# First norm of a two-layer diffusion trunk: whose engine makes the low parts of the first weight chunks, and in which order VectorE and TensorE take the tiles

## The chip, the cores and the metric

One core of one Trainium2 chip runs the whole program. The metric is the device time of one execution in microseconds (us). Names used here: TensorE (PE in the profile, PEld its weight loads), VectorE (DVE), ScalarE (ACT), GpSimd (POOL), and SyncE (SP), which issues most of the DMAs.

## The reference, cut to what matters

Two trunk layers on 256 latent and 256 context tokens of width 1024. Each layer is a half-step SwiGLU, a token mixer and a second half-step SwiGLU. Ahead of each stands an RMS norm with an adaptive shift and scale, which are themselves products of a conditioning vector with a weight matrix:

```python
ml = _split_mod(cond_lat @ mod_w[i] + mod_b[i])
mc = _split_mod(cond_ctx @ mod_w[i] + mod_b[i])
h = h + 0.5 * ml[2] * _swiglu(_modulate(h, ml[0], ml[1]), ffn1_w13[i], ffn1_w2[i])

def _modulate(h, shift, scale):
    return _rms(h) * (1.0 + scale) + shift
def _swiglu(h, w13, w2):
    a, b = jnp.split(h @ w13, 2, axis=-1)
    return (jax.nn.silu(a) * b) @ w2
```

The place of the change is the very first `_modulate` and the first columns of `h @ w13` behind it.

## The kernel before, in words

Activations lie transposed: eight tiles (k = 0 to 7) of 128 partitions (features) by 512 columns (256 latent, 256 context tokens). Every operand of a large product is split in two fp32r parts, a high part (a rounded copy) and a low part ("rest", the value less the high part), and each product is made of three: high weight by high x (`wh`, `xh`), low weight by high x (`wl`, `xh`), high weight by low x (`wh`, `xl`). ScalarE makes the high parts (casts), VectorE the rests (subtractions). Weights come in chunks of 1024 rows by 256 columns, each in two pieces of 128 x 1024 elements. Chunks 0 and 1 (the first pair) and chunk 2 are loaded before the steady loop begins. Chunks 0 and 1 are cut by halves of the rows: pieces 0 and 1 (rows 0 to 511, first gate and first value columns) lie in `raw`, pieces 2 and 3 (rows 512 to 1023) in `modw`; chunk 2 goes to `extra_hi` and `extra_lo` (inside `uh`).

The first norm runs tile by tile, and four engines take part in each tile k:

- `start_products(k)` on VectorE: two column sums (L872, two inputs of 128 x 1024 from SBUF) that make the scale of tile k, and a small operation (L1004) that finishes it.
- `start_tile(("shift", k))` on TensorE: eight fp32 products of two columns each (L1473, 16 instructions in the trace) that make the shift of tile k. `start_shift(k)` on VectorE (L1013) takes it out of PSUM.
- `start_tile(k)` on VectorE (L1037): x tile times the spread norm factors. It reads one operand in SBUF and one in PSUM.
- ScalarE: `xh` of tile k (L653, two halves), then the same in full precision in `tmp` (L659, two halves).
- `start_lo(k)` on VectorE (L1045): `xl` = `tmp` less `xh`, two inputs in SBUF.
- `start_products(k)` on TensorE: 12 products of 512 columns (L1486 and L1487 in turn, then four of L1492, which need `xl`).

TensorE's own order is: spread of the factors (L1676), shift sum of tile 1, then for each k: shift sum of tile k + 1, the 12 products of tile k. The order on every engine is the order of the code; engines meet at counting semaphores. `hi_ready` counts casts of weight pieces, `lo_ready` rests. GpSimd has only one thing to do in this stage, the root of the norm factors (L498), and behind it the fetches of the next modulation weights into `modw` (L522), which wait for `lo_ready` of 4 because pieces 2 and 3 lie in the same memory.

Behind the norm comes the "up" stage: chunk 2 (`extra_hi`, `extra_lo`), chunk 3, and then a loop over pairs of chunks, about 22 us each. In its first pair VectorE makes four column sums on the fetched modulation weights (`late_unit`), then the products of the two branches (L1164), their rests (L1169) and the rests of chunk 3 (L860).

Of the kernel before, what the change touches and what calls it, by code (L numbers as in the profile page):

```python
# [6 lines left out]
ALU = mybir.AluOpType  # L7
ACT = mybir.ActivationFunctionType
AX = mybir.AxisListType
F32 = mybir.dt.float32  # L10
# [156 lines left out]
def trunk(nc, tokens, columns, cond_rows, row_params, mod_start, mod_rows, f1_w13, f1_w2, f2_w13, f2_w2,  # L167
# [8 lines left out]
    with ExitStack() as stack:  # L176
# [313 lines left out]
        def _(pool):  # L490
# [14 lines left out]
            for ph in phases:  # L505
# [3 lines left out]
                elif kind == "norm" and ph["n"] == 0:  # L509
                    pool.wait_ge(ones_ready, 2)  # L510
                    root(0, slice(0, TT))
                elif kind == "norm":
                    for half in range(ph["T"] // LAT):
                        root(ph["st"] + half, slice(half * LAT // P, (half + 1) * LAT // P))
# [45 lines left out]
        def _(act):  # L560
# [78 lines left out]
            for n_ph, ph in enumerate(phases):  # L639
# [3 lines left out]
                if kind == "norm":  # L643
                    n, m0 = ph["n"], ph["L"] * MODT + 3 * ph["sub"] * DT
                    if n == 0:
                        for k in range(DT):
# [16 lines left out]
                            if k >= DT - 2:  # L663

                                p = k - (DT - 2)
# [185 lines left out]
        def _(dve):  # L851
# [11 lines left out]
            def start_pieces(p):  # L863
                for s in range(2):
                    cut = slice(p * DT // 2, (p + 1) * DT // 2)
                    dve.wait_ge(hi_ready, 2 * p + s + 1)
                    nc.vector.tensor_tensor(flat(wl[:, s, cut]), modw_slot[:, s] if p else raw[:, s, :],
                                            flat(wh[:, s, cut].bitcast(F32)), ALU.subtract).then_inc(lo_ready, 1)

# [154 lines left out]
            for n_ph, ph in enumerate(phases):  # L1024
# [9 lines left out]
                elif kind == "norm" and ph["n"] == 0:  # L1034
# [3 lines left out]
                    def extra_rest(p):  # L1038
                        half = slice(p * DT // 2, (p + 1) * DT // 2)
                        dve.wait_ge(hi_ready, 5 + p)  # L1040
                        nc.vector.tensor_tensor(flat(extra_lo[:, half]), raw[:, p, :], flat(extra_hi[:, half].bitcast(F32)),
                                                ALU.subtract).then_inc(lo_ready, 1)
# [4 lines left out]
                    start_pieces(0)  # L1047
                    start_products(1)
# [3 lines left out]
                    for k in range(1, 3):  # L1052
                        start_tile(k)
                    for k in range(1, DT):
                        start_shift(k)
                        start_lo(k - 1)
                        if k == 3:
                            start_pieces(1)
                        if k + 1 < DT:
                            start_products(k + 1)  # L1060
                        if k + 2 < DT:
                            start_tile(k + 2)
                        if k == DT - 1:
                            extra_rest(0)
                    start_lo(DT - 1)
                    extra_rest(1)
# [66 lines left out]
                elif kind == "up":  # L1133
# [6 lines left out]
                    def pair(i, units, unit_first=False):  # L1140
# [30 lines left out]
                        rest(2 * (q0 + i + 1) + 1, 1, late=late)  # L1171
                    pair(0, False, unit_first=ph["units"] > 0)
# [726 lines left out]
```

## Time and profile before

| | us |
|---|---|
| median of 3 runs | 1901.37 (1899.33 to 1901.51) |
| the profiled execution | 1904.52 |
| its span, first to last instruction | 1902.6 |
| TensorE busy | 1850.8 (97% of the span) |
| VectorE busy | 1185.4 (62%) |
| ScalarE busy | 687.8 (36%) |
| GpSimd busy | 149.6 (8%) |

The span is divided by stage in the trace; the stage of the change is its first 63 us. The granted clock of TensorE has two levels, 2.4 GHz (shown as 1.00) and 1.2 GHz. A matmul of 512 columns starts every 0.23 us at the high level and every 0.43 us at the low one. Over the span the mean is 0.987.

### The profile page before, as it was taken

How to read it: one execution, taken by the hardware profiler on the slowest of the kernel's cores; microseconds unless marked ns; L12 is line 12 of the kernel's file. 1: busy time of each engine (PE TensorE's matmuls, PEld its weight loads, DVE VectorE, ACT ScalarE, POOL GpSimd, SP SyncE). 2: the span in 40 equal slices, each digit the busy share in tenths (PEclk: the TensorE clock that was granted, in tenths of full speed). 3: DMA queues.
4: the chain of work that ended last, by engine and by line, in shares of the span. 5: the costliest groups of instructions: out<-in, count | busy, mean ns of one | idle time of the engine just before them, and what ended most of it. 6: DMA issues, size and time to landing. Idle time of an engine off the chain costs nothing.

```text
span 1902.6 us, 27442 instructions
## 1 busy us (share of the span) xinstructions
PE 1850.8 (97%) x9984; PEld 1587.8 (83%) x9984; DVE 1185.4 (62%) x1898; ACT 687.8 (36%) x1152; POOL 149.6 (8%) x228
## 2 busy tenths in 40 slices
PE   8999999999989999999999999999999989989997
PEld 6888888898966888888889888888898879978886
DVE  7877772355478478777424887752377445667764
ACT  5332232233258243223223322322254323545552
POOL 0010000100301200011001001000100000010000
PEclk9999999999999999999999999999999989999999
DMA  8466643334510246565233566533343213545554
GB/s 320 148 206 196 194 150 107 92 106 158 145 55 1 67 155 199 189 196 184 91 104 98 178 213 195 187 113 92 99 151 108 69 46 111 177 155 177 193 167 127
DMA packets 81886, 271.85 MB, mean 143 GB/s; under 512 B 9489, under 2 KB 14865, under 8 KB 81809
## 3 DMA queue, kind: packets, MB, share of 16 engines
q1 hardware_dynamic: 62354, 201.58, 32.4%
q0 software_dynamic: 19456, 69.22, 12.1%
q8 instruction: 52, 0.85, 0.2%
q14 instruction: 24, 0.20, 0.0%
HBM read 267.62 MB, written 1.05 MB: 141 GB/s over the span
## 4 chain that ended last, share of the span: by engine, by line
PE 90%; DVE 5%; issue 2%; ACT 2%; DMA 1%; SPq 0%; POOL 0%; POOLq 0%; DVEq 0%; ACTq 0%
PE pt L1429 19%; PE pt L1430 19%; PE pt L1432 19%; PE pt L1404 9%; PE pt L1403 4%; PE pt L1622 2%; PE pt L1839 2%; PE pt L1841 2%; PE pt L1840 2%; DVE wl L860 1%; PE pt L1502 1%; PE pt L1626 1%; PE pt L1566 1%; PE pt L1721 1%; PE pt L1568 1%
## 5 line engine op out<-in xcount | busy, mean ns | idle before, releaser
L860 DVE TENSOR_TENSOR wl<-raw,wh 128x1024 fp32r<-128x1024 f32 (+2 forms) x394 | 432.0, 1135 | 411.6 <-ACT wh L571 407.3
L1429 PE MATMUL pt<-xh,wh 128*128 128x512 f32 (+1 forms) x1312 | 496.5, 378 | 3.3 <-DVE wl L860 3.1
L1430 PE MATMUL pt<-xh,wl 128*128 128x512 f32 (+1 forms) x1312 | 495.2, 377 | 0.0
L1432 PE MATMUL pt<-xl,wh 128*128 128x512 f32 (+1 forms) x1312 | 493.8, 377 | 0.0
L571 ACT CAST wh<-raw 128x1024 fp32r<-128x1024 f32 (+2 forms) x394 | 364.2, 970 | 281.5 <-PE pt L1432 148.5
L872 DVE CUSTOM_DVE_ANT_0 pt<-modw,raw 128x1024 f32<-128x1024 f32 x256 | 305.7, 1253 | 17.4 <-DMA modw<-in_mod_rows 17.3
L1429 PEld LDWEIGHTS pt<-xh,wh 128*128 128x128 f32 x1312 | 248.4, 189 | 48.5 <-issue 3.7
L1432 PEld LDWEIGHTS pt<-xl,wh 128*128 128x128 f32 x1312 | 248.3, 189 | 45.5
L1430 PEld LDWEIGHTS pt<-xh,wl 128*128 128x128 f32 x1312 | 248.5, 189 | 44.6
L720 ACT CAST uh<-tmp 128x512 f32 (+3 forms) x88 | 49.7, 567 | 293.3 <-DVE tmp L1164 284.8
L1430 PE MATMUL pt<-uh,wl 128*128 128x512 f32 x396 | 154.1, 389 | 0.0
L1429 PE MATMUL pt<-uh,wh 128*128 128x512 f32 x396 | 154.1, 389 | 0.0
L1432 PE MATMUL pt<-ul,wh 128*128 128x512 f32 x396 | 154.1, 389 | 0.0
L1404 PE MATMUL pt<-xh,wh 128*128 128x512 f32 x352 | 121.7, 399 | 2.2 <-issue 2.2
L522 POOL DMA_DIRECT2D modw<-in_mod_rows x128 | 68.0, 531 | 642.4 <-DVE small L872 617.5
L710 ACT ACTIVATE tmp<-pt 128x512 f32<-128x512 f32 x66 | 39.1, 597 | 184.9 <-PE pt L1432 181.9
L1430 PEld LDWEIGHTS pt<-uh,wl 128*128 128x128 f32 x396 | 74.4, 188 | 15.5
L1432 PEld LDWEIGHTS pt<-ul,wh 128*128 128x128 f32 x396 | 74.3, 188 | 15.4
L1429 PEld LDWEIGHTS pt<-uh,wh 128*128 128x128 f32 x396 | 74.3, 188 | 15.3
L1403 PE MATMUL pt<-xh,wl 128*128 128x256 f32 x308 | 86.3, 280 | 0.0
L504 POOL TENSOR_TENSOR tmp<-tmp 128x512 f32<-128x512 f32 (+1 forms) x36 | 39.8, 1106 | 582.7 <-ACT tmp L578 582.5
L1404 PEld LDWEIGHTS pt<-xh,wh 128*128 128x128 f32 x352 | 63.7, 190 | 14.7 <-issue 2.5
(222 smaller groups left out, 2782.5 us busy)
## 6 DMA issues: line engine op xcount, KB each, us to landing
raw<-in_ffn_w SPq DMA_DIRECT2D x238, 512.0 KB, 4.0
modw<-in_mod_rows POOLq DMA_DIRECT2D x128, 512.0 KB, 4.6
raw<-in_ret_w_in SPq DMA_DIRECT2D x48, 512.0 KB, 4.5
raw<-in_diff_w_in SPq DMA_DIRECT2D x24, 512.0 KB, 4.4
raw<-in_ffn_w SPq DMA_DIRECT2D x32, 256.0 KB, 3.9
raw<-in_ret_w_out SPq DMA_DIRECT2D x16, 512.0 KB, 4.4
region<-in_mod_rows SPq DMA_DIRECT2D x8, 512.0 KB, 14.6
region<-in_mod_start SPq DMA_DIRECT2D x8, 512.0 KB, 15.0
```

The lines of the kernel that those rows point to most:

```text
L504: nc.gpsimd.tensor_tensor(ssq[:, 0:T], ssq[:, 0:T], tmp[:, e % 2, 0:T], ALU.add).then_inc(sq_added, 1)
L522: pool.dma_start(modw_slot[:, e], src).then_inc(mod_landed[e], 16)
L571: nc.scalar.copy(flat(wh[:, s, k0:k0 + part_rows]), raw[:, slot, 0:part_rows * CW]).then_inc(hi_ready, 1)
L710: nc.scalar.activation(tmp[:, t, 0:T], pt[:, t, 0:T], ACT.Silu).then_inc(evac[0], 1)
L720: nc.scalar.copy(row(uh, 2 * i + t)[:, 0:T], tmp[:, 2 + t, 0:T]).then_inc(u_hi_done, 1)
L860: nc.vector.tensor_tensor(flat(wl[:, s, cut]), raw[:, raw_slot(late, s, p), 0:part_rows * CW], flat(wh[:, s, cut].bitcast(F32)), ALU.subtr ...
L872: return nc.vector.tensor_tensor_reduce(products[j], weights, cond_row[:, j, :], 1.0, 0.0, ALU.mult, ALU.add, dst)
L1403: nc.tensor.matmul(bank[:, 0:LAT], w_lo, both[:, 0:LAT], start=False, stop=False)
L1404: ins = nc.tensor.matmul(bank, w_hi, both, start=a, stop=b)
L1429: nc.tensor.matmul(bank, w_hi[:, k, cut], hi(k), start=a, stop=False)
L1430: nc.tensor.matmul(bank, w_lo[:, k, cut], hi(k), start=False, stop=False)
L1432: return nc.tensor.matmul(bank, w_hi[:, k, cut], lo(k), start=False, stop=b)
```

## The change

The six rests of the pieces of chunks 0, 1 and 2 move from VectorE to GpSimd, as 128 x 1024 subtractions behind its root. VectorE normalises tile 0 as soon as the factors are spread, ahead of the column sums for tile 1, and then each tile k + 1 ahead of the column sums for tile k + 1. TensorE makes the four `wh` by `xh` products of a tile first, then the four `wl` by `xh`. ScalarE casts the two pieces of chunk 2 one tile earlier. VectorE waits for all six rests before its first own one.

```diff
                     pool.wait_ge(ones_ready, 2)
                     root(0, slice(0, TT))
+                    for p in range(2):
+                        for s in range(2):
+                            cut = slice(p * DT // 2, (p + 1) * DT // 2)
+                            pool.wait_ge(hi_ready, 2 * p + s + 1)
+                            nc.gpsimd.tensor_tensor(flat(wl[:, s, cut]), modw_slot[:, s] if p else raw[:, s, :],
+                                                    flat(wh[:, s, cut].bitcast(F32)), ALU.subtract).then_inc(lo_ready, 1)
+                    for p in range(2):
+                        half = slice(p * DT // 2, (p + 1) * DT // 2)
+                        pool.wait_ge(hi_ready, 5 + p)
+                        nc.gpsimd.tensor_tensor(flat(extra_lo[:, half]), raw[:, p, :], flat(extra_hi[:, half].bitcast(F32)),
+                                                ALU.subtract).then_inc(lo_ready, 1)
...
-                            if k >= DT - 2:
+                            if k in (DT - 3, DT - 2):
 
-                                p = k - (DT - 2)
+                                p = k - (DT - 3)
                                 act.wait_ge(raw_landed[p], 16 * raw_count(False, 1, 0))
...
-                    start_pieces(0)
-                    start_products(1)
                     dve.wait_ge(bcast_ready, 1)
                     start_tile(0)
                     start_shift(0)
-                    for k in range(1, 3):
-                        start_tile(k)
+                    start_tile(1)
+                    start_products(1)
                     for k in range(1, DT):
                         start_shift(k)
                         start_lo(k - 1)
-                        if k == 3:
-                            start_pieces(1)
                         if k + 1 < DT:
+                            start_tile(k + 1)
                             start_products(k + 1)
-                        if k + 2 < DT:
-                            start_tile(k + 2)
-                        if k == DT - 1:
-                            extra_rest(0)
                     start_lo(DT - 1)
-                    extra_rest(1)
...
+                    if q0 == 0:
+                        dve.wait_ge(lo_ready, 6)
                     pair(0, False, unit_first=ph["units"] > 0)
...
             def start_products(d):
 
                 halves = TOK // LAT
+                p = d // (DT // 2)
+                pe.wait_ge(hi_ready, 2 * p + 2)
+                pe.wait_ge(x_hi_done, halves * (d + 1))
                 for s in range(2):
-                    pe.wait_ge(lo_ready, 2 * (d // (DT // 2)) + s + 1)
-                    if s == 0:
-                        pe.wait_ge(x_hi_done, halves * (d + 1))
                     for t in range(2):
                         cut, bank = slice(t * P, (t + 1) * P), pt[:, 2 * s + t, :]
                         nc.tensor.matmul(bank, wh[:, s, d, cut], xh[:, d, :], start=(d == 0), stop=False)
+                for s in range(2):
+                    pe.wait_ge(lo_ready, 2 * p + s + 1)
+                    for t in range(2):
+                        cut, bank = slice(t * P, (t + 1) * P), pt[:, 2 * s + t, :]
                         nc.tensor.matmul(bank, wl[:, s, d, cut], xh[:, d, :], start=False, stop=False)
```

On GpSimd's queue, behind the root, the fetches of modulation weights stood next before:

```order
L498 TENSOR_TENSOR small<-small 128x4
L522 DMA modw<-in_mod_rows 128x1024
L522 DMA modw<-in_mod_rows 128x1024
L534 UNCONDITIONAL_BRANCH
L534 ISA
```

and stand behind the six rests now:

```order
L498 TENSOR_TENSOR small<-small 128x4 [waits var_ready,ones_ready]
L516 TENSOR_TENSOR wl<-raw,wh 128x1024 [waits hi_ready] x2
L516 TENSOR_TENSOR wl<-modw,wh 128x1024 [waits hi_ready] x2
L521 TENSOR_TENSOR uh<-raw,uh 128x1024 [waits hi_ready] x2
L533 DMA modw<-in_mod_rows 128x1024 [waits lo_ready]
L533 DMA modw<-in_mod_rows 128x1024
```

So both fetches are issued only after the last rest of chunk 2.

On VectorE's queue, from the scale of tile 0 to the low part of tile 0, this stood before (`region<-region,raw` is a column sum, `wl<-raw,wh` a rest, `region<-hT,pt` a normalised tile, `modT<-pt,cols_in` a shift):

```order
L1004 TENSOR_SCALAR sc<-small,cols_in 128x2
L867 TENSOR_TENSOR wl<-raw,wh 128x1024 x2
L872 ISA region,small<-region,raw 128x1024
L872 ISA small 128x1
L872 ISA region,small<-region,raw 128x1024
L872 ISA small 128x1
L1004 TENSOR_SCALAR sc<-small,cols_in 128x2
L1037 TENSOR_TENSOR region<-hT,pt 128x512
L1013 TENSOR_SCALAR modT<-pt,cols_in 128x2
L1037 TENSOR_TENSOR region<-hT,pt 128x512 x2
L1013 TENSOR_SCALAR modT<-pt,cols_in 128x2
L1045 TENSOR_TENSOR xl<-tmp,xh 128x512
```

and this stands there now:

```order
L1008 TENSOR_SCALAR sc<-small,cols_in 128x2
L1041 TENSOR_TENSOR region<-hT,pt 128x512
L1017 TENSOR_SCALAR modT<-pt,cols_in 128x2
L1041 TENSOR_TENSOR region<-hT,pt 128x512
L876 ISA region,small<-region,raw 128x1024
L876 ISA small 128x1
L876 ISA region,small<-region,raw 128x1024
L876 ISA small 128x1
L1008 TENSOR_SCALAR sc<-small,cols_in 128x2
L1017 TENSOR_SCALAR modT<-pt,cols_in 128x2
L1044 TENSOR_TENSOR xl<-tmp,xh 128x512
```

The two rests are gone, the first tile and its shift stand ahead of the column sums of tile 1, and the low part still stands behind the shift of the next tile.

## Rows read from the trace of the kernel before

**Rows 1.** Granted clock and busy time by stretch (engines' us, PEclk, DMA share, GB/s).

```profile
40.00:50.00 10.00, 9.41 (x38) 7.64 (x37) 8.76 (x20) 4.15 (x8) 0.00 (x0) 0.71 0.26 101
```

**Rows 2.** Timeline of TensorE, tiles 0 and 1: start us, us, line, operation.

```profile
19.59 3.54 PE L1473 MATMUL pt<-cond,region 128*128 128x2 f32 x16
24.17 0.77 PE L1486 MATMUL pt<-xh,wh 128*128 128x512 f32 x1 [1.03 <-ACT xh L653]
...
28.37 1.84 PE L1473 MATMUL pt<-cond,region 128*128 128x2 f32 x16
30.07 0.47 PE L1486 MATMUL pt<-xh,wh 128*128 128x512 f32 x1
...
32.00 1.09 PE L1492 MATMUL pt<-xl,wh 128*128 128x512 f32 x4
32.92 1.84 PE L1473 MATMUL pt<-cond,region 128*128 128x2 f32 x16
```

**Rows 3.** Timeline of TensorE, end of tile 3 to chunk 2.

```profile
40.85 0.39 PE L1487 MATMUL pt<-xh,wl 128*128 128x512 f32 x1
41.82 1.19 PE L1492 MATMUL pt<-xl,wh 128*128 128x512 f32 x4 [0.58 <-DVE xl L1045]
42.85 2.20 PE L1473 MATMUL pt<-cond,region 128*128 128x2 f32 x16
44.91 0.77 PE L1486 MATMUL pt<-xh,wh 128*128 128x512 f32 x1
...
50.18 2.24 PE L1473 MATMUL pt<-cond,region 128*128 128x2 f32 x16
...
62.64 0.47 PE L1429 MATMUL pt<-xh,uh 128*128 128x512 f32 x1
```

**Rows 4.** Timeline of VectorE: column sums, tile, rests.

```profile
14.47 1.23 DVE L872 CUSTOM_DVE_ANT_0 region<-region,raw 128x1024 f32<-128x1024 f32 x1
...
25.65 1.22 DVE L872 CUSTOM_DVE_ANT_0 region<-region,raw 128x1024 f32<-128x1024 f32 x1
...
28.19 0.68 DVE L1037 TENSOR_TENSOR region<-hT,pt 128x512 f32<-128x512 f32 x1
...
35.54 2.36 DVE L867 TENSOR_TENSOR wl<-modw,wh 128x1024 fp32r<-128x1024 f32 x2
```

**Rows 5.** Timeline of ScalarE: high part of tile 0, casts of pieces 2 and 3.

```profile
22.93 1.09 ACT L653 ACTIVATE xh<-region,modT,sc 128x256 fp32r<-128x256 f32 x2 [5.14 <-DVE modT L1013]
...
32.54 1.97 ACT L629 CAST wh<-modw 128x1024 fp32r<-128x1024 f32 x2
```

**Rows 6.** GpSimd's groups by shape: busy us, mean ns, idle before.

```profile
L504 POOL TENSOR_TENSOR tmp<-tmp 128x512 f32<-128x512 f32 x24 | 31.0, 1291 | 333.6 <-ACT tmp L578 333.4
L504 POOL TENSOR_TENSOR tmp<-tmp 128x256 f32<-128x256 f32 x12 | 8.8, 736 | 249.1 <-ACT tmp L578 249.1
```

**Rows 7.** Timeline of GpSimd at 632 us, and VectorE's L860 there.

```profile
632.86 2.73 POOL L504 TENSOR_TENSOR tmp<-tmp 128x512 f32<-128x512 f32 x2 [10.45 <-ACT tmp L578]
...
L860 DVE TENSOR_TENSOR wl<-raw,wh x1: 2144/2144/2144, 634.5 to 634.5; 128x1024 fp32r<-128x1024 f32 x1
```

**Rows 8.** VectorE's L860 over the whole span: ns min/median/max, first and last start.

```profile
L860 DVE TENSOR_TENSOR wl<-raw,wh x394: 410/1219/2144, 69.7 to 1884.8; 128x1024 fp32r<-128x1024 f32 x197
```

**Rows 9.** GpSimd's root of 128x4 elements, and the eight others of its shape.

```profile
14.65 1.91 POOL L498 TENSOR_TENSOR small<-small 128x4 f32<-128x4 f32 x1 [13.54 <-DVE small L892]
...
L554 POOL TENSOR_TENSOR small<-small x8: 1006/1008/1030, 566.9 to 620.9; 128x4 f32<-128x4 f32 x8
```

**Rows 10.** One of those eight, and VectorE beside it.

```profile
576.00 1.01 POOL L554 TENSOR_TENSOR small<-small 128x4 f32<-128x4 f32 x1 [8.09 <-DVE small L1302]
...
575.84 0.74 DVE L1315 SCALAR_TENSOR_TENSOR xl<-pt,small,xh 128x512 fp32r<-128x512 f32 x1
```

**Rows 11.** Fetches of modulation weights: GpSimd's timeline, and their landing.

```profile
38.21 1.27 POOL L522 DMA_DIRECT2D modw<-in_mod_rows  x2 [21.64 <-DVE wl L867]
...
modw<-in_mod_rows POOLq DMA_DIRECT2D x2, 512.0 KB, 4.4
```

More of the change, by code:

```diff
@@ L861, in rest @@
                                             flat(wh[:, s, cut].bitcast(F32)), ALU.subtract).then_inc(lo_ready, 1)
[L863 to L868, printed above, removed]
             def column_sum(dst, weights, j, products):
@@ L1037, in start_tile @@
                         nc.vector.tensor_tensor(start_sq[k], hT[:, k, :], pt[:, BC, :], ALU.mult).then_inc(normed, 1)
[L1038 to L1042, printed above, removed]
                     def start_lo(k):
```

## The prediction

> **What bounds the kernel now.** I read the chain of waits first: 90% of it is TensorE, so what TensorE gains by 62.64 us, where chunk 2 begins, it keeps to the end, as long as nothing behind is late. Then the stretches: the stage of the change holds one with a low clock, 0.71 on average from 40 to 50 us [rows 1]. Then TensorE's timeline. A full tile has a pitch of 4.55 us (28.37 to 32.92): 1.70 for the shift sum of the next tile and 2.85 for the 12 products, of which the last four, which need `xl`, begin 1.93 after the first [rows 2]. Against that pitch three things are lost. (a) TensorE is free at 23.13 (19.59 + 3.54) and waits 1.03 for `xh` of tile 0 [rows 2]. (b) At tile 3 the last `wl` product starts at 40.85, so `xl` is due at 41.08; it comes at 41.82: 0.74 [rows 3]. (c) Behind this stall and the nearly empty shift sum TensorE runs at 1.2 GHz: the 12 products of tile 4 take 5.27 (44.91 to 50.18) instead of 2.85, the two shift sums around them 2.20 and 2.24 instead of 1.84 [rows 2, 3], together 3.2.
>
> Why is VectorE late at tile 3? Its work per tile is 2.54 for the column sums (25.65 to 28.19 [rows 4]), about 0.60 each for tile and low part (half of a 1024 rest) and 0.13 for the shift: 3.9 of the 4.55. That leaves it 0.7 in hand, and the two rests at 35.54 take 2.3 [rows 4]. Other rests stand where VectorE waits anyway.
>
> **The change part by part.** *Start.* VectorE no longer makes two rests and the sums of tile 1 before tile 0. The factors are spread when TensorE turns to the shift sum at 19.59, so `xh` is ready at about 21.7 (0.7 for tile and shift, 1.1 on ScalarE [rows 2, 5]), before 23.13. TensorE starts 1.03 earlier; part of that is spent in products at the low clock, which I expect to rise at the same moment as before. I take -0.6; the bound is -1.03.
>
> *Rests off VectorE.* Without them VectorE keeps the pace, and (b) and (c) go: -0.74 and -3.2. With the start -4.5, the most this change can bring (-5.0 with the bound above).
>
> *Rests on GpSimd.* 128x256 takes it 736 ns, 128x512 1291 [rows 6], 555 for each 256 elements, so 128x1024 should take 2.40, six of them 14.4. GpSimd has nothing else to do here. By its own clock the rests are in time: pieces 2 and 3 are cast by about 33.9 and would be ready at 38.7, and the `wl` products of tile 4 need them at about 44.
>
> But the two engines do not work side by side. At 634.53 VectorE's L860 starts while GpSimd is in the second of two additions of 128x512, which end at 635.59 (632.86 + 2.73). It takes 2144 ns [rows 7] where the median is 1219 [rows 8]: 0.93 more for 1.06 of overlap. The other way round, GpSimd's root, started 0.18 after a column sum, takes 1.91, and operations of its shape take 1.01 [rows 4, 9]; 0.9 is what was left of the column sum. Beside a VectorE operation with one input in PSUM GpSimd isn't delayed (1.01 [rows 10]). So I read: GpSimd's two-input operations and VectorE's operations on two SBUF inputs exclude each other, each waits for the end of the other's instruction, and normalised tiles and shifts run on. Column sums and low parts, 3.1 of VectorE's 3.9 per tile, are of the kind that waits. The Trainium skill says the same in its GPSIMD Engine Reference, section Specifications: the SBUF interfaces are shared with VectorE, with contention when that has two SBUF inputs. By its figure of 4497 ns for 2048 elements (section Performance versus the Vector engine) a rest would be an estimated 2.25; the sum uses 2.40.
>
> I follow the timetable with this rule; t(k) is the time at which TensorE turns to the products of tile k - 1. Tile 0 ends at about 27.8 (28.37 - 0.6), so t(2) = 27.8 + 1.7 = 29.5 and t(3) = 29.5 + 4.55 = 34.05. The first two rests fall where VectorE waits for the spread and cost it 0.5 with room to spare. The third starts at 33.2, behind a column sum, and ends at 35.65. VectorE wants the low part of tile 2 at 34.3 and gets it at 36.2; it is due at 34.05 + 1.93 = 35.98: stall 0.2. The fourth rest follows to 38.5 and holds the column sums of tile 4, which end at 41.0; the low part of tile 3 stands behind them and is there at 41.85, due at t(4) + 1.93 = 38.8 + 1.93 = 40.7: stall 1.15. VectorE catches up at tile 4. The fifth rest (cast at 48.3, run 48.85 to 51.25) puts the low part of tile 5 at 51.75 against 51.0: stall 0.8. The sixth (cast 52.3) falls among the column sums of tile 7, and the low part of tile 6 comes at 58.0 against 56.3: stall 1.75. Sum of the stalls +3.9; tile 7 ends at about 61.8. Bounds: 0 if the engines run side by side, and 6.5 if VectorE must let two rests in a row pass (2.4 more at tile 2, with a little recovered at tile 3).
>
> *Clock.* In the trace a stall of 0.74 beside a shift sum was followed by one low stretch worth 3.2. The new timetable has three stalls of that size or larger beside a shift sum, so I expect one low stretch again. But while TensorE is slow VectorE catches up, and one or two of the later stalls shrink by about 2.0 together. Net +1.2; bounds 0 (none) and 6.4 (two stretches, nothing recovered).
>
> *Order on TensorE, casts.* The `wh` products in front make `wl` due 0.9 later; it isn't what is late in the walk. The casts of chunk 2 fill ScalarE's idle time and end before the fifth and sixth rests need them. Both cost nothing; if `wl` of tile 4 were late after all, the four `wh` products cover 0.9.
>
> *Fetches.* They stand behind six rests now and are issued at 56 instead of 38.21 (1.27 for both), and land 4.4 later [rows 11], at about 61.5. The four column sums of the first up pair then end near 66.5, chunk 3's first rest near 70.5, due at 61.8 + 0.24 + 48 x 0.2275 = 73.0. The cover is about 2.5; the price nothing now, one for one beyond it. VectorE's new wait for six rests ends earlier than the landing. SyncE's loads of chunk 3 wait for rests 5 and 6, which come at 51 and 56 and so no later than before.
>
> Sum against the profiled execution (1904.52, span 1902.6): -4.5 + 3.9 + 1.2 = +0.6. The profile is 3.15 above the median of the timed runs, which is close to what its low stretch cost. If timed runs mostly lack that stretch, their start is only 1.3 better than now at best, and the same new stalls and one stretch make +3.8 (-1.3 + 3.9 + 1.2). I take a value nearer to the profile than to this end: +1.0, so 1902.4.
>
> **The rivals.** 0.2 per cent (3.8 us) is about what a measurement of this kernel tells from no change.
>
> Likeliest (0.60): exclusion as above, the stall on `xl` moved from one place to three or four. 1902.4, its own range 1899.5 to 1905.5.
>
> Side by side (0.20): GpSimd's long subtractions pass between VectorE's operations, TensorE has no stall, no low stretch: 1901.4 - 4.5 = 1896.9, or 1900.1 against runs that had no low stretch. For it: GpSimd is idle here. Against it: 2144 against 1219.
>
> Clock falls twice (0.15), the one on the slower side: the stalls of 1.15 and 1.75 are each followed by a low stretch, whose 3.2 is not recovered because the second comes last. 1901.4 - 4.5 + 3.9 + 6.4 = 1907.2. It decides from a second stretch on; for it speaks that the new stalls are longer than the 0.74 that was followed by one, against it that stretches overlap stalls.
>
> Late fetches (0.05): exclusion delays the rests and so the fetches by 5 more, over the cover of 2.5: TensorE waits 2.5 at chunk 3, 1904.9.
>
> **How the numbers follow.** Faster by over 0.2% is the better half of side by side plus an edge of the likeliest: 0.15. Slower is the two falls and an edge of the likeliest and of late fetches: 0.18. The rest, 0.67, is within 0.2%. The range leaves out half of side by side and half of the two falls: 1898.0 to 1905.8.
>
> **What would show it.** In the profile after: the six rests at 2.4 each or longer; column sums or low parts on VectorE with 2 to 3 us instead of 1.22 and 0.68 where a rest overlaps; TensorE waiting for `xl` at tiles 2, 3, 5 and 6; `xh` of tile 0 no longer waited for; chunk 2 begun at 61 to 63. The prediction is wrong if VectorE's maxima stay at 1.2 and chunk 2 begins near 58, or if GpSimd's rests stretch over 5 us and TensorE waits for `wl`.

## The result, and the profile after

| | before | after |
|---|---|---|
| median, us (20 runs each) | 1901.26 (1898.72 to 1904.71) | 1906.34 (1902.05 to 1910.43) |
| ratio of after to before | | 1.0022, 95% interval 1.0015 to 1.003 |
| profiled execution, us | 1904.52 | 1907.78 |
| its span, us | 1902.6 | 1905.8 |
| chunk 2 begins at, us | 62.64 | 65.77 |
| GpSimd busy, us | 149.6 | 164.5 |
| VectorE busy, us | 1185.4 | 1189.4 |

The changed kernel is slower, by 0.22 per cent by the ratio, which is just over what this measurement can tell from no change; the medians lie 5.1 apart (0.27 per cent). Its runs fall in two groups, 9 from 1902.05 to 1903.75 and 11 from 1906.24 to 1910.43, and the profile is from the second. Two of the rows need a word. GpSimd's 14.9 more are the six subtractions. VectorE's busy time has grown although its work shrank: time in which an instruction of VectorE is held by GpSimd counts as its busy time.

In the two profiles the whole loss lies ahead of chunk 2: it begins 3.13 later and the span is 3.2 longer. TensorE's timeline of the changed kernel, stage of the change:

```profile
19.83 3.54 PE L1466 MATMUL pt<-cond,region 128*128 128x2 f32 x16 [0.17 <-DMA region<-in_mod_start]
23.24 2.05 PE L1479 MATMUL pt<-xh,wh 128*128 128x512 f32 x4
...
27.78 1.84 PE L1466 MATMUL pt<-cond,region 128*128 128x2 f32 x16
...
35.05 1.07 PE L1484 MATMUL pt<-xh,wl 128*128 128x512 f32 x4
38.51 1.20 PE L1489 MATMUL pt<-xl,wh 128*128 128x512 f32 x4 [2.39 <-DVE xl L1044]
39.54 2.48 PE L1466 MATMUL pt<-cond,region 128*128 128x2 f32 x16
41.88 2.05 PE L1479 MATMUL pt<-xh,wh 128*128 128x512 f32 x4
...
47.14 1.96 PE L1466 MATMUL pt<-cond,region 128*128 128x2 f32 x16
...
55.87 1.20 PE L1489 MATMUL pt<-xl,wh 128*128 128x512 f32 x4 [0.27 <-DVE xl L1044]
...
61.74 1.19 PE L1489 MATMUL pt<-xl,wh 128*128 128x512 f32 x4 [1.04 <-DVE xl L1044]
...
65.77 0.47 PE L1422 MATMUL pt<-xh,uh 128*128 128x512 f32 x1
```

It answers to [rows 2, 3]. `xh` of tile 0 is no longer waited for: the second shift sum starts at 27.78 instead of 28.37. Tile 2 waits for `xl` until 38.51, where it was due at 34.04 + 1.93 = 35.97: 2.5 lost. Tiles 5 and 6 lose 0.4 and 1.2 more by the same count. Behind the longest stall TensorE falls to its lower clock, and the 12 products of tile 3 take 5.26 (41.88 to 47.14) instead of 2.85. By stretch, the granted clock stands in the column behind the five engines, and answers to [rows 1]:

```profile
30.00:40.00 10.00, 7.61 (x44) 6.30 (x43) 9.96 (x11) 6.01 (x10) 4.84 (x2) 1.00 0.91 361
40.00:50.00 10.00, 10.00 (x46) 8.66 (x46) 6.36 (x16) 2.63 (x6) 0.00 (x0) 0.66 0.00 2
```

In the first stretch TensorE is busy for 7.61 of 10 and VectorE for 9.96 with 11 instructions; in the second it is the other way round, VectorE has 3.6 to spare. GpSimd's timeline says what ran beside it:

```profile
16.56 4.83 POOL L516 TENSOR_TENSOR wl<-raw,wh 128x1024 fp32r<-128x1024 f32 x2
33.06 4.84 POOL L516 TENSOR_TENSOR wl<-modw,wh 128x1024 fp32r<-128x1024 f32 x2 [11.67 <-ACT wh L640]
52.54 2.54 POOL L521 TENSOR_TENSOR uh<-raw,uh 128x1024 fp32r<-128x1024 f32 x1 [14.63 <-ACT uh L678]
58.40 2.55 POOL L521 TENSOR_TENSOR uh<-raw,uh 128x1024 fp32r<-128x1024 f32 x1 [3.32 <-ACT uh L678]
60.89 1.27 POOL L533 DMA_DIRECT2D modw<-in_mod_rows  x2
```

And VectorE's timeline, at the third and fourth rest and at the first fetched weights:

```profile
33.40 2.21 DVE L1008 TENSOR_SCALAR sc<-small,cols_in 128x2 f32<-128x2 f32 x1
35.53 0.21 DVE L1017 TENSOR_SCALAR modT<-pt,cols_in 128x2 f32<-128x2 f32 x1
35.66 2.79 DVE L1044 TENSOR_TENSOR xl<-tmp,xh 128x512 fp32r<-128x512 f32 x1
...
66.92 1.23 DVE L876 CUSTOM_DVE_ANT_0 pt<-modw,raw 128x1024 f32<-128x1024 f32 x1 [2.34 <-DMA modw<-in_mod_rows]
```

The third rest starts at 33.06 beside a column sum that ends at 33.36. The next instruction on VectorE is the small one that finishes a scale (L1008, 128 x 2 elements, one tensor input): it starts at 33.40 and is held until the third rest ends at 35.5. The shift (L1017, input in PSUM) takes its usual 0.21. Then the fourth rest has begun, and the low part, which TensorE waits for, is held for its whole length: 2.79 instead of 0.68. The three other rests that meet a scale (the first, the fifth and the sixth) hold it the same way. The group view of L1008 and L1044 (ns minimum/median/maximum):

```profile
L1008 DVE TENSOR_SCALAR sc<-small,cols_in x8: 228/1208/2229, 16.9 to 58.7; 128x2 f32<-128x2 f32 x8
...
L1044 DVE TENSOR_TENSOR xl<-tmp,xh x8: 674/682/2795, 23.9 to 63.3; 128x512 fp32r<-128x512 f32 x8
```

The fetches leave at 60.89, VectorE waits 2.34 for what they bring, and chunk 3 begins without a wait all the same. At no place of this stage does TensorE wait for `wl`, so GpSimd is not simply too slow.

### The profile page after: what moved, and what is told of

Its sections match the earlier page's. It is cut to its first block, busy times and chain, and to the rows that moved or that the text cites. A ratio compares the mean times of both kernels' runs of the same rounds, so it can differ in the third digit from the quotient of the medians.

```text
span 1905.8 us, 27443 instructions
## 1 busy us (share of the span) xinstructions
PE 1851.5 (97%) x9984; PEld 1587.6 (83%) x9984; DVE 1189.4 (62%) x1892; ACT 688.1 (36%) x1152; POOL 164.5 (9%) x234
## 4 chain that ended last, share of the span: by engine, by line
PE 89%; DVE 5%; issue 2%; ACT 2%; DMA 1%; SPq 0%; POOL 0%; POOLq 0%; DVEq 0%; ACTq 0%
PE pt L1422 19%; PE pt L1425 19%; PE pt L1423 19%; PE pt L1397 9%; PE pt L1396 4%; PE pt L1619 2%; PE pt L1836 2%; PE pt L1838 2%; PE pt L1837 2%; DVE wl L871 1%; PE pt L1499 1%; PE pt L1623 1%; PE pt L1563 1%; PE pt L1718 1%; PE pt L1565 1%
## 6 DMA issues: line engine op xcount, KB each, us to landing
region<-in_mod_start SPq DMA_DIRECT2D x8, 512.0 KB, 14.9
```

## The experiments

All ratios are to the kernel before, run beside each experiment. Diffs are against the changed kernel, unless said otherwise, and show only the lines that matter. The theory is the one on record: GpSimd's and VectorE's instructions exclude each other, and each pays with whole instructions. The rivals: the loss comes from the new order on VectorE or TensorE; GpSimd is simply too slow; the fetches come too late. Each run has one trace, so what is read from a trace is read from one execution.

**The new order with no work on GpSimd.** All six rests back on VectorE, one at a time: two while it waits for the spread factors, one each after tiles 2 and 4, and the two of chunk 2 after tiles 6 and 7.

```diff
+                    start_rest(0)
+                    start_rest(1)
                     dve.wait_ge(bcast_ready, 1)
...
+                        if k in (2, 4):
+                            start_rest(1 + k // 2)
+                        if k >= DT - 2:
+                            extra_rest(k - (DT - 2))
```

> Exclusion theory (GpSimd's long two-input operations stop VectorE): the changed kernel with all six rests back on VectorE, the first two while it waits for the spread factors, the others one per tile (behind tiles 2 and 4, two at the end). VectorE is at most 0.6 us late at any tile, so TensorE has no stall over 0.3 us between tile 0 and chunk 2, no low stretch of the clock, and chunk 2 begins at about 58.0 (62.64 before, 65.77 in the changed kernel). Time: 1.3 to 4.6 us under before, 7 to 8 under the changed kernel in the profile. Rival (the new order is what costs, or the two engines do run side by side and the rests are just late): no faster than the changed kernel, chunk 2 at 65 or later, because VectorE has 7 us more to do. Clock rival: stalls go but a low stretch stays, chunk 2 at 61.

Measured: 1898.69 (1896.72 to 1901.44, 11 runs), ratio 0.9983 (0.9974 to 0.9992), so 0.17 per cent faster than the kernel before. TensorE never waits once it is going, its clock stays at the higher level once it has risen, and chunk 2 begins at 58.35. The stretch from 40 to 50 us, where the changed kernel has a granted clock of 0.66:

```profile
40.00:50.00 10.00, 10.00 (x62) 8.86 (x61) 9.84 (x19) 6.03 (x13) 1.27 (x2) 1.00 0.28 105
```

VectorE, which is now busy for 9.84 of 10, was never short of time for the rests; it was short of it for two in a row. So the new order isn't the loss: the same order without GpSimd's subtractions is ahead of both kernels.

**The same with the rests in pairs**, where the kernel before has them (both of pieces 2 and 3 after the low part of tile 2).

```diff
+                        if k == 3:
+                            start_rest(2)
+                            start_rest(3)
```

> The changed kernel with the rests on VectorE in pairs where the kernel before had them (two together behind the low part of tile 2, the last two around the low part of tile 7). Exclusion theory: the stall at tile 3 of before comes back (0.5 to 0.8 us) with or without one low stretch behind it (3.2 us), the start is 0.6 to 1.0 earlier, chunk 2 begins at 59 to 62; time 0.5 to 2 us under before and 4 to 5 under the changed kernel. Rival (the new order costs): about the changed kernel's time. It also tells what spreading the rests is worth by itself, against the run with single rests.

Measured: 1900.61, ratio 0.9993 (0.9983 to 1.0002; one run far outside left out). The stall at tile 3 is back, as [rows 3] have it, but here without a low stretch behind it, and chunk 2 begins at 59.03 (TensorE's timeline):

```profile
41.40 1.20 PE L1497 MATMUL pt<-xl,wh 128*128 128x512 f32 x4 [0.58 <-DVE xl L1046]
42.44 1.84 PE L1474 MATMUL pt<-cond,region 128*128 128x2 f32 x16
44.14 1.17 PE L1487 MATMUL pt<-xh,wh 128*128 128x512 f32 x4
```

Pairs against single rests: 0.7 of stall in the trace, 1.9 between the medians, with intervals that overlap. A stall of 0.58 beside a shift sum was followed by the low level in the trace of before and not in this one.

**GpSimd's rests in quarters.** Each 128 x 1024 subtraction becomes four of 128 x 256, on the same engine, in the same place.

```diff
+                    def rest_parts(dst, src, hi):
+                        for a in range(0, PIECE, PIECE // 4):
+                            ins = nc.gpsimd.tensor_tensor(dst[:, a:a + PIECE // 4], src[:, a:a + PIECE // 4],
+                                                          hi[:, a:a + PIECE // 4], ALU.subtract)
+                        ins.then_inc(lo_ready, 1)
```

> The changed kernel with each GpSimd rest cut in four subtractions of 256 elements (0.74 us each, 17.7 in sum instead of 14.7). Exclusion that goes by whole instructions: VectorE gets in between the quarters, no VectorE operation is longer than about 2.0 us (2.79 in the changed kernel), the low part of tile 2 comes 1 to 2 us earlier and the stall at tile 2 shrinks from 2.5 to 0.5 to 1.5; time 1 to 3 us under the changed kernel. Rival (GpSimd slows VectorE by sharing bandwidth, not by turns): VectorE's operations are stretched by the same total, more work for GpSimd, time as the changed kernel or up to 1 us above it.

Measured: 1902.54, ratio 0.9999 (0.999 to 1.0008), 4.4 under the changed kernel by the ratios, more than expected. An instruction of VectorE is now held for some 0.5 at most, and GpSimd gives way in its turn: eight quarters take 9.68 where two whole rests took 4.84 and eight of 0.736 [rows 6] would be 5.9 (GpSimd's timeline, then VectorE's).

```profile
33.82 9.68 POOL L514 TENSOR_TENSOR wl<-modw,wh 128x256 fp32r<-128x256 f32 x8 [9.50 <-ACT wh L644]
```

```profile
34.16 0.57 DVE L1012 TENSOR_SCALAR sc<-small,cols_in 128x2 f32<-128x2 f32 x1
...
40.00 1.18 DVE L1048 TENSOR_TENSOR xl<-tmp,xh 128x512 fp32r<-128x512 f32 x1
```

TensorE's stall at tile 2 is gone, the one at tile 6 is 0.42, chunk 2 begins at 59.60. The profile is from one of the three shortest runs (1898.70), so it shows less than the median has. What the change pays for is the length of GpSimd's instruction, not its speed. But in this kernel the fetches, issued at 56.76 behind rests that take longer, are no longer free. At chunk 3 TensorE waits, and VectorE has waited for the fetched weights before (TensorE's timeline, then VectorE's):

```profile
71.59 0.50 PE L1426 MATMUL pt<-xh,wh 128*128 128x512 f32 x1 [0.82 <-DVE wl L875]
```

```profile
62.70 1.23 DVE L880 CUSTOM_DVE_ANT_0 pt<-modw,raw 128x1024 f32<-128x1024 f32 x1 [4.68 <-DMA modw<-in_mod_rows]
```

**Quarters, and the first two fetches ahead of the rests of chunk 2.** The diff shows the fetches alone; the quarters are those of the run above.

```diff
...
+                    pool.wait_ge(lo_ready, 4)
+                    for e in range(2):
+                        pool.dma_start(modw_slot[:, e], mod_rows[0, 2 * START_UNITS + e]).then_inc(mod_landed[e], 16)
                     for p in range(2):
                         half = slice(p * DT // 2, (p + 1) * DT // 2)
```

> The run with quartered rests again, with the two first fetches of modulation weights ahead of the rests of chunk 2 instead of behind them. In that run VectorE waited 4.7 us for the fetched weights and TensorE 0.8 at chunk 3. Theory (the late fetch is a second price, hidden in the changed kernel by its late TensorE): the wait for the fetched weights goes, the stall at chunk 3 goes, time 0.5 to 1.5 us under the quartered run. Rival (the stall at chunk 3 is due to something else, such as SyncE's loads behind rests 5 and 6): it stays at 0.8.

Measured: 1900.73 (1896.54 to 1903.24), ratio 0.9994 (0.9985 to 1.0003). The fetches leave at 43.73, both waits are gone, and chunk 2 begins at 59.53. The span (1897.5) isn't shorter than that of the quarters alone (1896.6), so in the profiles the 0.82 isn't seen in the end; the medians differ by 1.8, with intervals that overlap. That the early fetch is worth time is not shown.

**What excludes what: a probe.** The kernel before, with unused GpSimd work added on free memory: four operations of 128 x 512 of each of four kinds, beside VectorE's steady work. It computes what the kernel before computes.

```diff
+                    for n in range(4):
+                        probed(nc.gpsimd.tensor_tensor(b, a, b, ALU.subtract))
...
+                        probed(nc.gpsimd.tensor_copy(b, a))
...
+                        probed(nc.gpsimd.tensor_scalar(b, a, 2.0, None, ALU.mult))
...
+                        probed(nc.gpsimd.memset(b, 1.0))
```

> The kernel before with work added to GpSimd that nothing uses, on free memory: after the scale of tile 2 four subtractions of 512 elements (two inputs), after that of tile 4 four copies (one input), after that of tile 5 four multiplications by a constant (one input), after that of tile 6 four fills (no input). Its time isn't compared; VectorE's column sums (1.22), low parts (0.68) and scales (0.23) beside each group are read. Exclusion by two inputs on GpSimd alone: only beside the subtractions are they longer, by 0.5 to 1.2 each; beside copies, multiplications and fills they keep their lengths. Wider exclusion (any GpSimd operation that reads SBUF): copies and multiplications do the same. Sharing of bandwidth: every kind stretches them a little, none by the rest of a GpSimd instruction.

Measured in one execution. GpSimd's timeline, then VectorE's: column sums (L894) beside each kind, and the scale (L1026) beside the fills:

```profile
28.28 6.54 POOL L524 TENSOR_TENSOR region<-region 128x512 f32<-128x512 f32 x4 [10.61 <-DVE sc L1026]
42.47 4.74 POOL L527 COPY region<-region 128x512 f32<-128x512 f32 x4 [7.64 <-DVE sc L1026]
47.42 7.03 POOL L530 TENSOR_SCALAR region<-region 128x512 f32<-128x512 f32 x4 [0.21 <-DVE sc L1026]
54.50 2.27 POOL L533 MEMSET region<- 128x512 f32 x4
```

```profile
31.38 2.31 DVE L894 CUSTOM_DVE_ANT_0 region<-region,raw 128x1024 f32<-128x1024 f32 x1
...
45.12 1.62 DVE L894 CUSTOM_DVE_ANT_0 region<-region,raw 128x1024 f32<-128x1024 f32 x1
...
53.02 1.62 DVE L894 CUSTOM_DVE_ANT_0 region<-region,raw 128x1024 f32<-128x1024 f32 x1
...
54.57 1.22 DVE L894 CUSTOM_DVE_ANT_0 region<-region,raw 128x1024 f32<-128x1024 f32 x1
...
55.83 0.38 DVE L1026 TENSOR_SCALAR sc<-small,cols_in 128x2 f32<-128x2 f32 x1
```

A column sum costs 1.22 alone. It costs 1.1 more beside subtractions, 0.4 more beside copies or multiplications by a constant (four of five; the one at 48.50, inside a multiplication, keeps 1.21), and nothing more beside fills. The low part at 47.87, also inside a multiplication (47.42 to 48.92), keeps 0.70. So a multiplication does not hold VectorE for its whole length, as a subtraction of 128 x 1024 did. The scale is the other way: it takes 0.23 alone and is held by the fills too (0.38). Shifts, which read PSUM, keep their 0.21 beside all four, and normalised tiles, which read one operand there, their 0.68 beside the first three (none fell beside the fills). So a one-input operation on GpSimd would not have been free either, and two kinds of VectorE operation are held, by different rules. Both theories of the expectation were too simple: copies and multiplications do hold VectorE, but for less than their length.

**GpSimd's rests alone.** The kernel before with only the six rests moved; VectorE's, TensorE's and ScalarE's order as before. The diff shows VectorE's start alone.

> One part of the change alone: the kernel before with the six rests on GpSimd and nothing else (orders of VectorE, ScalarE and TensorE as before). Exclusion theory: VectorE, relieved of 7 us of rests, still loses 2.2 to 2.8 us at its scale and low part when rests 3 and 4 run, TensorE stalls 1.5 to 2.7 us at tile 2 or 3 and again at tiles 6 or 7 (casts of chunk 2 one tile later), chunk 2 begins at 64 to 67; time 2 to 5 us over before, like the whole change. Rival (the new orders are what costs): chunk 2 no later than 62.6 and time at or under before's.

```diff
+                    start_products(1)
                     dve.wait_ge(bcast_ready, 1)
...
-                    start_tile(1)
-                    start_products(1)
+                    for k in range(1, 3):
+                        start_tile(k)
```

Measured: 1913.02 (1909.27 to 1914.09, 5 runs), ratio 1.0055 (1.0041 to 1.0069), the slowest of all, 10 over the kernel before where 2 to 5 were expected; chunk 2, at 65.86, is where it was expected. TensorE's timeline shows three losses:

```profile
25.83 0.77 PE L1493 MATMUL pt<-xh,wh 128*128 128x512 f32 x1 [3.00 <-ACT xh L664]
...
44.81 1.21 PE L1499 MATMUL pt<-xl,wh 128*128 128x512 f32 x4 [1.22 <-DVE xl L1056]
...
80.58 0.50 PE L1436 MATMUL pt<-xh,wh 128*128 128x512 f32 x1 [3.60 <-DVE wl L871]
81.29 0.63 PE L1439 MATMUL pt<-xl,wh 128*128 128x512 f32 x1
```

The wait for the first `xh` has grown from 1.03 to 3.00, because a column sum of tile 1, ahead of tile 0 on VectorE, is held for a rest (19.16, 3.20). And the last rest comes at 63.43, the fetches at 65.77, the first rest of chunk 3 3.60 too late; the eight products from 80.92 to 84.28 run at the lower clock (1.5 more than at 0.23 each). Chunk 2 begins 3.2 later, and 3.2 + 3.6 + 1.5 = 8.3 is most of the span's 9.4. The rows say that tile 0 first takes away the wait of 3.00. That the earlier casts are what brings the fetches in time is argued, since all the old orders come back here together.

**The first two rests on GpSimd, the other four on VectorE**, one at a time, as in the first experiment.

```diff
+                    for s in range(2):
+                        pool.wait_ge(hi_ready, s + 1)
+                        nc.gpsimd.tensor_tensor(flat(wl[:, s, 0:DT // 2]), raw[:, s, :],
+                                                flat(wh[:, s, 0:DT // 2].bitcast(F32)), ALU.subtract).then_inc(lo_ready, 1)
```

> The run with single rests on VectorE, but the first two on GpSimd, which makes them while VectorE waits for the spread factors. Exclusion theory: they hold the scale of tile 0 (2.2 instead of 0.23) and the first column sum of tile 1 (1.4 instead of 1.2), all of it within time that VectorE has; no stall on TensorE, chunk 2 at 58.0 to 58.6, time within 0.5 us of the run with all rests on VectorE. Rival (any rest on GpSimd costs, by slower VectorE or later low weights): 1 us or more over that run.

Measured: 1897.64 (1896.3 to 1899.85), ratio 0.9984 (0.9975 to 0.9993). The two rests still hold a scale (2.20) and a column sum (1.45), but where VectorE has time; nothing stalls and chunk 2 begins at 57.69. It can't be told from the first experiment (0.9983) by its time.

**Unused products in TensorE's wait.** The changed kernel with 16 products of 256 columns, whose results nobody reads, ahead of the `xl` products of tile 2.

```diff
+                for n in range({2: 8}.get(d, 0)):
+                    nc.tensor.matmul(pt[:, (SUM, 4, 5)[d % 3], 8:LAT + 8], wh[:, 0, d, 0:P], xh[:, d, 0:LAT], start=True, stop=True)
+                    nc.tensor.matmul(pt[:, (SUM, 4, 5)[d % 3], 8:LAT + 8], wh[:, 0, d, P:2 * P], xh[:, d, 0:LAT], start=True, stop=True)
```

> The changed kernel with 16 products of 256 columns (1.8 us at the high clock) that nothing uses, on TensorE in its wait for the low part of tile 2, which was 2.5 us. Clock theory: the low stretch behind that stall cost about 3 us, and with TensorE kept at work it isn't entered: the 12 products of tile 3 take 2.8 us instead of 5.3, chunk 2 begins 1 to 3 us earlier (later stalls grow, since VectorE no longer catches up), the median is 1 to 3 us under the changed kernel's and the timed runs lie closer together. Rival (the low stretch comes from the shift sums or from the power of the products, not from the stall): it stays, and the filler costs nothing or up to 0.5 us.

Measured: 1903.09 (1900.68 to 1906.44), ratio 1.0006 (0.9997 to 1.0015). The stall is there, of its 2.6 some 1.9 are filled, and the clock doesn't fall at tile 3; but it falls at tile 6, behind a wait of 0.30 at tile 5. TensorE's timeline, then two stretches:

```profile
39.51 1.19 PE L1492 MATMUL pt<-xl,wh 128*128 128x512 f32 x4 [0.56 <-DVE xl L1044]
...
42.24 1.17 PE L1479 MATMUL pt<-xh,wh 128*128 128x512 f32 x4
...
56.45 2.04 PE L1479 MATMUL pt<-xh,wh 128*128 128x512 f32 x4
58.28 1.83 PE L1484 MATMUL pt<-xh,wl 128*128 128x512 f32 x4
```

```profile
40.00:50.00 10.00, 10.00 (x65) 8.86 (x63) 9.43 (x20) 4.80 (x9) 0.00 (x0) 1.00 0.00 1
50.00:60.00 10.00, 9.70 (x51) 8.11 (x51) 9.44 (x13) 4.31 (x9) 6.28 (x4) 0.83 0.19 57
```

So the low stretch at tile 3 hung on TensorE's idle time and not on its lateness, and it has a price of its own. The later one costs 1.6 here (56.45 to 59.95 for eight products, 1.93 at the higher clock), but TensorE doesn't wait at tile 6 any more. Chunk 2 begins at 63.86, and by the ratios the filler wins 3.0. The timed runs agree: one of these 11 has a mean granted clock of 0.988 or below, the profiled one, and 10 of the changed kernel's 20.

**The fourth rest behind the low part of tile 2.** It keeps the two rests from following each other.

```diff
+                            if (p, s) == (1, 1):
+                                pool.wait_ge(x_ready, 3)
```

> The changed kernel, but GpSimd's fourth rest waits until VectorE has made the low part of tile 2. In the changed kernel the small scale operation took VectorE's turn between rests 3 and 4, and the low part had to wait for the fourth as well (2.79 us). Turn theory: the low part of tile 2 comes at about 36.3, the stall at tile 2 shrinks from 2.5 to 0.2 to 0.5, the fourth rest now holds the column sums of tile 4 instead and a stall of 0.7 to 1.5 appears at tile 3; chunk 2 begins 0.5 to 2 us earlier than in the changed kernel at the same number of low stretches, time 0.5 to 2.5 us under it. Rival (the sum of GpSimd's time beside VectorE is what counts, whatever the turns): the stall of 2.5 moves whole to tile 3, time unchanged.

Measured: 1904.11 (1901.19 to 1906.11), ratio 1.0012 (1.0003 to 1.0021). TensorE's timeline, then VectorE's:

```profile
37.32 1.20 PE L1491 MATMUL pt<-xl,wh 128*128 128x512 f32 x4 [0.27 <-DVE xl L1046]
...
43.06 1.19 PE L1491 MATMUL pt<-xl,wh 128*128 128x512 f32 x4 [0.91 <-DVE xl L1046]
44.09 1.84 PE L1468 MATMUL pt<-cond,region 128*128 128x2 f32 x16
45.79 1.74 PE L1481 MATMUL pt<-xh,wh 128*128 128x512 f32 x4
```

```profile
36.59 0.68 DVE L1046 TENSOR_TENSOR xl<-tmp,xh 128x512 fp32r<-128x512 f32 x1
...
37.79 3.08 DVE L878 CUSTOM_DVE_ANT_0 region<-region,raw 128x1024 f32<-128x1024 f32 x1
```

At tiles 2 and 3 this is the timetable of the prediction: tile 2 loses 0.4, tile 3 1.1 (due at 41.98), the low part of tile 2 takes its 0.68 and the fourth rest holds a column sum instead. Tile 5 loses nothing and tile 6 0.4. Chunk 2 begins at 62.87, 2.9 earlier than with the change as it is, although the second shift sum starts 0.6 later (28.36): there the clock rose later. Not all of the 2.9 belongs to the turn: the stalls are 1.9 together instead of 4.2, and the low stretch, now at tile 4, costs 1.6 instead of 3.2 (45.79 to 50.22 for 12 products). By the ratios the run wins 1.9, with intervals that overlap.

**The first experiment with TensorE's products in their old order.**

> The run with single rests on VectorE, with TensorE's order as before (high and low weight products in turn instead of the four high ones first). With the low weights ready in time the order of products is worth nothing: no stall, chunk 2 at 58.0 to 58.6, time within 0.5 us of the run with single rests. Rival (the leading high-weight products cover a late rest, of tile 4 above all, whose last rest ends 0.5 us after TensorE turns to it): TensorE waits 0.3 to 1 us at tile 4, and a low stretch of the clock may follow; 1 to 3 us slower.

```diff
                 for s in range(2):
+                    pe.wait_ge(lo_ready, 2 * (d // (DT // 2)) + s + 1)
+                    if s == 0:
+                        pe.wait_ge(x_hi_done, halves * (d + 1))
```

Measured: 1898.23 (1895.99 to 1901.79), ratio 0.9983 (0.9974 to 0.9992), the same as with the new order; chunk 2 begins at 58.39 against 58.35. `wh` products in front are worth nothing here.

## Why it came out as it did

The mechanism was in the main the predicted one, and the time came out above the predicted 1902.4: the median by 3.9, which is 0.5 over the upper end of the range, and 1.0022 times the 1901.4 that the prediction started from by 3.2, which is inside it. The prediction had given 0.18 to a loss over 0.2 per cent. Step by step:

- **Start, -0.6.** Right: 28.37 became 27.78. The clock rises where it did before, so of the 0.93 by which tile 0 starts earlier (23.24 against 24.17) a third is spent at the lower level.
- **The old stall and its low stretch, -0.74 and -3.2.** Right as a bound: with the rests one at a time on VectorE (first experiment) chunk 2 begins 4.3 earlier, where the prediction's sum is 4.5. This needed nothing from GpSimd.
- **Exclusion.** Right for what it names: column sums and low parts are held by whole subtractions, and the run with quarters shows that the length of the instruction is the price. But the step said that only operations on two SBUF inputs wait. **This is the step that failed.** The scale of 128 x 2 elements has one tensor input, and takes 2.2 beside a rest. It matters at tile 2: the scale waited for the third rest, the low part behind it met the fourth, and the stall came out as 2.5 where the walk had 0.2 there and 1.15 at tile 3. With the fourth rest held back the walk's two numbers are nearly there (0.4 and 1.1). The Trainium skill has the rule that the prediction left out. In its page SBUF — State Buffer, section Who interferes with whom, copies and `tensor_scalar` operations can run in a mode that takes both of VectorE's port pairs, and then exclude any GpSimd instruction, while an operation on two SBUF inputs contends with one that reads SBUF, not with one that only writes it; in that mode whoever starts first keeps the ports for its whole instruction. The traces agree in who meets whom: scale 2.21 and a copy of 128 x 8 elements 2.27 beside rests (the latter in the run with GpSimd's rests alone), column sum unchanged and scale 0.38 beside fills, shift 0.21 throughout. They don't bear out a hold for the whole length beside every operation of GpSimd: the probe's multiplication lets a low part of 0.70 and a column sum of 1.21 pass.
- **Walk of the stalls, +3.9.** The sum was near, 4.2 measured, but by luck: its parts were 0.2, 1.15, 0.8 and 1.75 at tiles 2, 3, 5 and 6, and 2.5, 0, 0.4 and 1.2 came, so 1.2 too little at the first two and 0.9 too much at the last two.
- **One low stretch, net +1.2.** It came, and cost 3.2 (2.4 in the products of tile 3, 0.6 and 0.1 in the two shift sums). The 2.0 that VectorE was to win back, for which the prediction has no working, didn't come. VectorE did catch up, with a wait of 3.12 at 49.14, but the fifth and sixth rests came after that, and a wait can't be stored: tile 5 loses 0.4 with this stretch and 0.45 in the run with the filler, which has none there. Where the stretch lies later it does win back: with the fourth rest held back, the fifth (49.46) falls inside it, and tiles 5 and 6 lose 0 and 0.4. This is the largest term that was mis-sized: net +3.2 for +1.2.
- **Order on TensorE and casts, 0.** Right for TensorE's order where the low weights are early, shown by the last experiment. The casts were not run alone; in the run without them (and with the old orders) the fetches came 5 later.
- **Fetches, 0.** Right for this kernel: VectorE waits 2.34 for them and TensorE doesn't wait at chunk 3. They were issued at 60.89 and not at 56, and were used from 66.92 on. The cover is thin. In the run with GpSimd's rests alone the first column sum on them starts at 71.70, and TensorE waited 3.60.

In the traces the sum so becomes -0.6 - 0.74 - 3.2 + 4.2 + 3.2 = +2.9, and 3.13 was measured at chunk 2. Over all runs the loss is larger, 4.2 by the ratio and 5.1 between the medians. The prediction had a second sum against timed runs that lack the old low stretch, +3.8, and took +1.0, nearer to the profile; the +3.8 was the better one. Grouped by the mean granted clock of a run:

| mean clock of the run | before, runs: mean us | after, runs: mean us |
|---|---|---|
| 0.991 | 31: 1900.1 | 6: 1902.3 |
| 0.989 | 30: 1902.0 | 3: 1904.6 |
| 0.987 | 9: 1904.6 | 7: 1909.1 |

(75 runs of before, from the comparisons of the experiments, and 20 of after; 5 and 4 of them lie at other values.) At the same clock the changed kernel is 2.2 to 4.5 behind, and of its runs 10 in 20 are at 0.988 or below, of the others 10 in 75. It is tempting to read each step of the mean clock as one more low stretch in this stage: then most timed runs of the kernel before had no such stretch, there was less of the 3.2 to win back than the sum took, and more new ones to add. This isn't shown, since timed runs have no timeline, and the profiles warn against it. All of them have low stretches far behind this stage too. The first and the last experiment show it best: chunk 2 begins at 58.35 and 58.39, neither has a low stretch ahead of it once the clock has risen, and yet their spans are 1896.9 and 1900.0 and their mean clocks 0.990 and 0.988. Two windows of both traces, from the first and then from the last:

```profile
540.00:560.00 20.00, 16.39 (x94) 9.79 (x94) 17.04 (x33) 16.47 (x51) 0.00 (x0) 0.91 0.16 53
...
540.00:560.00 20.00, 16.15 (x78) 9.64 (x79) 15.89 (x29) 14.58 (x41) 0.00 (x0) 0.83 0.16 53
```

So 3 us between two profiles of this program can come from behind chunk 2, and only the start of chunk 2, the ratios and their intervals say something of the change.

The rivals: side by side is refuted by the held scales and low parts. Late fetches did not happen in this kernel and did in two others. Clock falls twice didn't happen in the profile, where one stretch follows the first stall and none the 1.2 at tile 6; its time, 1907.2, is within a microsecond of the measured median, for another reason.

**What stays open.** Whether a stall is followed by the lower clock isn't settled by its length. By the idle time in the traces, of the waits for `xl` that have a shift sum behind them, those of 0.30 (filler, tile 5), 0.58 (before), 0.91 (fourth rest held back), 1.02 (probe), 1.22 (GpSimd's rests alone) and 2.39 were, and those of 0.27 (twice), 0.56 (filler, tile 2) and 0.58 (rests in pairs) weren't. The four at tile 6, which has no shift sum behind it, weren't either (0.27, 0.40, 0.42 and 1.04). Whether the shift sum is the reason was not tested. Nor was the timed runs' share of low stretches in this stage.

## What to carry to other kernels

Work moved to an idle GpSimd isn't free when VectorE works beside it: price it by how long one instruction of GpSimd is, and look at what stands on VectorE when it starts, the smallest SBUF-only operation included. Two long operations in a row on either engine cost most (0.58 on VectorE, 2.39 on GpSimd), while single ones on GpSimd still cost 0.4 and 1.2; the same work spread by one per tile on VectorE beat both kernels (1898.7, or 1897.6 with the first two on GpSimd where VectorE waits anyway). And an engine that catches up during a slow stretch wins back only what its late work inside the stretch would have cost.

## What the runs showed of the hardware that was not expected

- A `tensor_scalar` of 128 x 2 elements in SBUF takes 0.23 alone and 2.19 to 2.23 beside a GpSimd subtraction of 128 x 1024; with its input in PSUM it takes 0.21 in either case.
- GpSimd's fill of 128 x 512 (0.52) leaves column sums at 1.22; its copy and its multiplication by a constant make four of five 1.62 or 1.63, though the multiplication itself lasts 1.50.
- Cutting a GpSimd subtraction into quarters lets both engines take turns: the longest low part falls from 2.79 to 1.18, while eight quarters stretch to 9.68 where two whole ones take 4.84.
- In one trace unused products in a stall of 2.6 kept the clock up behind it, and a wait of 0.30 some 14 us later was then followed by a low stretch.
